# Even mixer's filling weight chunks as split fp32r pieces instead of fp32 tiles

## The reference

```python
def even_mixer(h, w_in, a_qn, a_kn, w_out, top_k):
    aq, ak, av, iq, ik, iw, bq, bk, bv, bg = split_cols(h @ w_in, EVEN_SIZES)
    ...
    ya = dsa_attention(aq, ak, hd(av, A_HEADS), hd(iq, IDX_HEADS), ik, iw, top_k)
    yb = retention(pad_left(hd(bq, B_HEADS)), pad_left(hd(bk, B_HEADS)),
                   pad_left(hd(bv, B_HEADS)))[:, META_PAD:]
    yb = rms_norm_2(yb).astype(h.dtype).reshape(B, L, -1) * jax.nn.silu(bg)
    return jnp.concatenate([ya, yb], axis=-1) @ w_out
```

## Time and profile before

| | us |
|---|---|
| median of 3 runs | 1893.85 (1892.3 to 1895.7) |
| the profiled execution | 1892.15 |
| its span in the trace | 1890.4 |
| TensorE busy | 1860.4 (98%) |
| VectorE busy | 1102.2 (58%) |
| ScalarE busy | 725.6 (38%) |
| TensorE's share of the chain that ended last | 88% |

### The profile page before, as it was taken

One profiled execution on the slowest core, in us unless ns is written; L12 is line 12 of the kernel. 1 busy time (PEld: TensorE's weight loads), 2 busy tenths in 40 slices (PEclk: granted clock), 3 DMA queues, 4 the chain that ended last, 5 costly groups with the idle time before them and its releaser, 6 DMA issues.

```text
span 1890.4 us, 31079 instructions
## 1 busy us (share of the span) xinstructions
PE 1860.4 (98%) x12732; PEld 1686.2 (89%) x12732; DVE 1102.2 (58%) x1752; ACT 725.6 (38%) x928; POOL 0.2 (0%) x4
## 2 busy tenths in 40 slices
PE   9999999999999999999999999999999999999999
PEld 6788999968899999999858558999999999789999
DVE  4556887544588856675344322567556764546763
ACT  3345554224465544333113222433343332334442
POOL 0000000000000000000000000000000000000000
PEclk9999999999999999999999999999999999999999
DMA  5322545424145544554322322345445453144553
GB/s 224 111 112 90 178 178 206 161 98 155 49 140 183 204 176 170 173 179 182 136 99 90 122 112 78 134 170 183 180 166 175 171 194 139 58 162 166 180 211 120
DMA packets 35859, 284.23 MB, mean 150 GB/s; under 512 B 4800, under 2 KB 6976, under 8 KB 8256
## 3 DMA queue, kind: packets, MB, share of 16 engines
q1 hardware_dynamic: 35776, 283.05, 41.8%
HBM read 281.98 MB, written 1.05 MB: 150 GB/s over the span
## 4 chain that ended last, share of the span: by engine, by line
PE 88%; DVE 7%; ACT 4%; issue 1%; DMA 0%; ACTq 0%; DVEq 0%; SPq 0%
PE PS L1192 18%; PE PS L1193 18%; PE PS L1194 18%; PE PS L639 10%; PE PS L648 3%; PE PS L747 3%; DVE split L1757 3%; PE PS L1095 2%; PE PS L616 2%; ACT split L1303 2%; PE PS L719 1%; PE PS L1136 1%; PE PS L662 1%; PE PS L682 1%; PE PS L923 1%
## 5 line engine op out<-in xcount | busy, mean ns | idle before, releaser
L1192 PE MATMUL PS<-Hhi,split 128*128 128x256 f32 (+1 forms) x2080 | 591.7, 284 | 8.6 <-DVE split L1757 7.9
L1757 DVE TENSOR_TENSOR split<-wa,split 128x2048 fp32r<-128x2048 f32 (+1 forms) x174 | 436.9, 2511 | 272.4 <-ACT split L1303 272.4
L1193 PE MATMUL PS<-Hlo,split 128*128 128x256 f32 (+1 forms) x2080 | 591.2, 284 | 0.0
L1194 PE MATMUL PS<-Hhi,split 128*128 128x256 f32 (+1 forms) x2080 | 589.3, 283 | 0.0
L1303 ACT CAST split<-wa 128x2048 fp32r<-128x2048 f32 (+1 forms) x174 | 361.9, 2080 | 145.8 <-PE PS L1194 145.1
L1192 PEld LDWEIGHTS PS<-Hhi,split 128*128 128x128 f32 x2080 | 391.7, 188 | 13.4 <-DVE split L1757 10.7
L1194 PEld LDWEIGHTS PS<-Hhi,split 128*128 128x128 f32 x2080 | 390.9, 188 | 0.0
L1193 PEld LDWEIGHTS PS<-Hlo,split 128*128 128x128 f32 x2080 | 390.6, 188 | 0.2
L1192 PE MATMUL PS<-hidhi,split 128*128 128x256 f32 (+1 forms) x1088 | 310.3, 285 | 6.4 <-DVE hidlo L2333 3.5
L1194 PE MATMUL PS<-hidhi,split 128*128 128x256 f32 (+1 forms) x1088 | 308.9, 284 | 0.0
L1193 PE MATMUL PS<-hidlo,split 128*128 128x256 f32 (+1 forms) x1088 | 308.1, 283 | 0.0
(11 more groups left out here) (283 smaller groups left out, 1696.1 us busy)
## 6 DMA issues: line engine op xcount, KB each, us to landing
wa<-in_wfi SPq DMA_DIRECT2D x126, 1024.0 KB, 4.8
wa<-in_wfo SPq DMA_DIRECT2D x48, 1408.0 KB, 5.8
wa<-in_wmix SPq DMA_DIRECT2D x26, 2048.0 KB, 7.9
wa<-in_wmix SPq DMA_DIRECT2D x4, 1536.0 KB, 6.3
H<-in_wfi SPq DMA_DIRECT2D x3, 1024.0 KB, 10.0
G<-in_wfi SPq DMA_DIRECT2D x3, 1024.0 KB, 4.9
wa<-in_wmix SPq DMA_DIRECT2D x2, 1024.0 KB, 5.9
wa<-in_wmix SPq DMA_DIRECT2D x2, 768.0 KB, 7.5
```

The lines of the kernel that those rows point to most:

```text
L1192: pe.matmul(o, hi, xhi, start=first, stop=False)
L1193: pe.matmul(o, hi, xlo, start=False, stop=False)
L1194: return pe.matmul(o, lo, xhi, start=False, stop=last)
L1757: dve.tensor_tensor(out=wlo[n % 2][:, 0:width], in0=wa[:, c % 2, 0:width], in1=whi[n % 2][:, 0:width].bitcast(F32), op=ALU.subtract).then_ ...
```

## The change

The six filling chunks are computed as split products. The host lays each of them out as four pieces of 8 x 128 columns, so that a piece is contiguous. ScalarE rounds H once into Ehi and VectorE subtracts into Elo, and for each of the 24 pieces ScalarE writes a high half (`round_piece`) into one of three places and VectorE writes the remainder over the weights themselves in wa (`rest_piece`, wa_lo is the same place as wa). TensorE waits for the remainder of the piece and runs `product3` over its 8 tiles: 24 fp32r matmuls. A high half's place is free again when the piece three before has been multiplied. The values are made like the others, channels on partitions, in four tiles of 272 tokens, copied over H by ScalarE and then turned by 12 transposes per group (jobs v0t and v1t). The chunks' order becomes rq, rk, v0, v1, gate0, gate1. The gates and the retention's result lie in RET, the place of QK, since Ehi and Elo take G's and MIX's. The orders of all three engines are rewritten around this. Cut to its core, with part of the indentation taken off deeply nested code:

```diff
-FILL = [(name, i) for name, n in (("rq", 4), ("rk", 4), ("v0", 3), ("turn_q", 4), ("turn_k", 4), ("gate0", 4), ("v1", 3),
-                                  ("gate1", 4)) for i in range(n)]
+FILL = [(name, i) for name, cols in (("rq", range(4)), ("rk", range(4)), ("v0", range(4)), ("turn_q", range(4)),
+                                     ("turn_k", range(4)), ("v1", range(4)), ("v0t", range(3)), ("gate0", range(4)),
+                                     ("gate1", range(2)), ("v1t", range(3)), ("gate1", range(2, 4))) for i in cols]
+SPLIT_EVEN = ("rq", "rk", "v0", "v1", "gate0", "gate1")
-EVEN_FREE = [None, None, None, ("dv_in", 3), None] + [filled(n) for n in ("rq", "rk", "v0", "gate0", "v1", "gate1")] + [None] * 2
+EVEN_FREE = [None, None, None, ("dv_in", 3), None] + [filled(n) for n in SPLIT_EVEN] + [None] * 2
...
+        def over(name, shape):
+            with ExitStack() as shared_place:
+                return shared_place.enter_context(nc.sbuf_tensor(name, shape, F32R))
+        wa_lo = over("wa_lo", [P, 2, KD * 512])
         wa = sb("wa", [P, 2, KD * 512])
...
+        rope_hi = over("rope_hi", [P, KD * P])
         rope = sb("rope", [P, 4, SEQ])
+        own_hi = sb("own_hi", [P, KD * P], F32R)
...
+        with ExitStack() as mix_ctx:
+            mix_ctx.enter_context(nc.sbuf_tensor("mix_head", [P, 4, TT], F32))
+            Elo = mix_ctx.enter_context(nc.sbuf_tensor("Elo", [P, KD, TT], F32R))
         MIX = sb("MIX", [P, 12, TT])
...
+        Ehi, RET = Hhi, QK
+        piece_hi = (split[:].rearrange("p a b -> p (a b)")[:, 10 * P * KD:11 * P * KD], own_hi[:], rope_hi[:])
...
         def ret_out(g):
-            return norm_plan(lane_b2, TT, 4, 0, MIX[:, 4 + 4 * g:8 + 4 * g, :], width=P, post=G[:, 4 * g:4 * g + 4, :])
+            return norm_plan(lane_b2, TT, 4, 0, RET[:, 4 * g:4 * g + 4, :], width=P, post=RET[:, 4 * g:4 * g + 4, :])
...
                     i, bank = FILL[f][1], f % 2
                         pe.wait_ge((S.ring0, S.ring1)[bank], f // 2)
-                    if name in ("v0", "v1"):
-                        mm = tokens(w, 0, 512, RETAINED[i:i + 1], [(bank, 0)])
+                    if name in ("v0t", "v1t"):
+                        last = FILL.index((name[:2], 3))
+                        pe.wait_ge((S.ring0, S.ring1)[last % 2], last // 2 + 1)
+                        pe.wait_ge((S.ring0, S.ring1)[1 - last % 2], (last - 1) // 2 + 1)
+                        t0, tl = RETAINED[i]
+                        for h in range(4):
+                            mm = pe.transpose(PS[0:tl, bank, P * h:P * h + P], H[:, 4 * (name == "v1t") + h, t0:t0 + tl], ident)
                     elif name in ("turn_q", "turn_k"):
                         mm = pe.matmul(PS[:, bank, 0:TT], C("rot", P), lane.QK[:, 4 * (name == "turn_k") + i, :], start=True,
                                        stop=True)
                     else:
-                        mm = tiles(w, [(P * i, P, bank)], TT)
+                        n = 4 * SPLIT_EVEN.index(name) + i
+                        pe.wait_ge(S.ev_lo, n + 1)
+                        hi = piece_hi[n % 3].rearrange("p (k c) -> p k c", k=KD)
+                        lo = wa_lo[:, w, KD * P * i:KD * P * (i + 1)].rearrange("p (k c) -> p k c", k=KD)
+                        for k in range(KD):
+                            mm = product3(PS[:, bank, 0:TT], hi[:, k, :], lo[:, k, :], Ehi[:, k, :], Elo[:, k, :], k == 0,
+                                          k == KD - 1)
                     mm.then_inc(S.fill_in, 1)
                     jobs[0] += 1
+                def slot(c):
+
+                    assert take() == base + c
+                    return (base + c) % 2
...
     def retained(g):
         pe.wait_ge(S.rt_m, upto(S.rt_m))
+        f = FILL.index((f"v{g}t", 2))
+        pe.wait_ge((S.ring0, S.ring1)[f % 2], f // 2 + 1)
+        pe.wait_ge((S.ring0, S.ring1)[1 - f % 2], (f - 1) // 2 + 1)
...
     tiles(use(4, base, KD, 512), [(P * i, P, at + i) for i in range(4)], TT).then_inc(S.prod_done, 1)
-    w = use(5, base, KD, 512)
+    w = slot(5)
+    pe.wait_ge(S.ev_xlo, 1)
     fill("rq", w)
     mean_square(k)
+    fill("rq", w)
     fill("rq", w)
...
     fill("rq", w)
     for a in dsa:
         attend_transposes(a, 0)
-    fill("rq", w)
+    w = slot(6)
+    fill("rk", w)
     for a in dsa:
         attend_scores(a, 1)
-    w = use(6, base, KD, 512)
     fill("rk", w)
     fill("rk", w)
...
-    fill("rk", w)
-    w = use(7, base, KD, 512)
-    fill("v0", w)
+    w = slot(7)
+    for _ in range(3):
+        fill("v0", w)
     for a in dsa:
         attend_transposes(a, 2)
     fill("v0", w)
     for a in dsa:
         pe.wait_ge(S.sm_ptc, upto(S.sm_ptc))
         attend_values(a)
-    fill("v0", w)
     for name in ("turn_q", "turn_k"):
         for _ in range(4):
             fill(name)
-    w = use(8, base, KD, 512)
-    fill("gate0", w)
-    fill("gate0", w)
+    w = slot(8)
+    for _ in range(3):
+        fill("v1", w)
     pe.wait_ge(S.pv_copied, upto(S.pv_copied, 2))
     pe.wait_ge(S.ret_ready, 1)
     decay_scores(0, 0)
-    fill("gate0", w)
+    fill("v1", w)
     decay_scores(0, 1)
+    for _ in range(3):
+        fill("v0t")
+    w = slot(9)
     fill("gate0", w)
     decay_scores(0, 2)
-    w = use(9, base, KD, 512)
-    fill("v1", w)
+    fill("gate0", w)
     retained(0)
-    fill("v1", w)
+    fill("gate0", w)
+    fill("gate0", w)
     mean_square(ret_out(0))
-    fill("v1", w)
-    w = use(10, base, KD, 512)
+    w = slot(10)
+    fill("gate1", w)
     pe.wait_ge(S.nr_rs, upto(S.nr_rs, 0))
-    for kt in range(3):
-        fill("gate1", w)
-        decay_scores(1, kt)
+    decay_scores(1, 0)
+    fill("gate1", w)
+    decay_scores(1, 1)
+    for _ in range(3):
+        fill("v1t")
+    fill("gate1", w)
+    decay_scores(1, 2)
     fill("gate1", w)
     retained(1)
     wo = [use(11, base, 12, 256)]
-    pe.wait_ge(S.ring0, 15)
-    pe.wait_ge(S.ring1, 15)
+    pe.wait_ge(S.ring0, 19)
+    pe.wait_ge(S.ring1, 19)
...
         for j in ks:
-            mm = pe.matmul(PS[:, m, 0:TT], wo[m // 2][:, j, P * (m % 2):P * (m % 2) + P], MIX[:, j, :],
+            mm = pe.matmul(PS[:, m, 0:TT], wo[m // 2][:, j, P * (m % 2):P * (m % 2) + P],
+                           MIX[:, j, :] if j < 4 else RET[:, j - 4, :],
                            start=j == 0, stop=j == 11)
...
         i, bank = FILL[f][1], f % 2
         act.wait_ge(S.fill_in, f + 1)
-        if name in ("v0", "v1"):
-            tl, g = RETAINED[i][1], name == "v1"
+        if name in ("v0t", "v1t"):
+            tl, g = RETAINED[i][1], name == "v1t"
             ins = act.copy(lane.VP[0:tl, i, 4 * g:4 * g + 4, :],
                            PS[0:tl, bank, :].rearrange("p (h d) -> p h d", h=4))
+        elif name in ("v0", "v1"):
+            ins = act.copy(H[:, 4 * (name == "v1") + i, :], PS[:, bank, 0:TT])
         elif name in ("gate0", "gate1"):
-            ins = act.activation(G[:, 4 * (name == "gate1") + i, :], PS[:, bank, 0:TT], ACT.Silu)
+            ins = act.activation(RET[:, 4 * (name == "gate1") + i, :], PS[:, bank, 0:TT], ACT.Silu)
         else:
             ins = act.copy(lane.QK[:, 4 * (name == "rk") + i, :], PS[:, bank, 0:TT])
         ins.then_inc((S.ring0, S.ring1)[bank], 1)
...
+                def round_piece(n):
+
+                    c = base + 5 + n // 4
+                    act.wait_ge(WA[c % 2], 16 * (c // 2 + 1))
+                    if n >= 3:
+                        act.wait_ge(S.fill_in, FILL.index((SPLIT_EVEN[(n - 3) // 4], (n - 3) % 4)) + 1)
+                    at = KD * P * (n % 4)
+                    act.copy(piece_hi[n % 3], wa[:, c % 2, at:at + KD * P]).then_inc(S.ev_hi, 1)
...
         relu()
+    act.copy(Ehi[:], H[:]).then_inc(S.ev_xhi, 1)
+    for n in range(3):
+        round_piece(n)
     product(base + 4)
     squares_of(k)
     filled_tile("rq")
+    round_piece(3)
     roots_of(k)
     filled_tile("rq")
+    round_piece(4)
+    filled_tile("rq")
+    round_piece(5)
     for a in dsa:
         attend_exp(a, 0)
...
         attend_copies(a, 0)
-    filled_tile("rq")
+    round_piece(6)
+    filled_tile("rk")
+    round_piece(7)
...
         attend_exp(a, 1)
     filled_tile("rk")
+    round_piece(8)
     filled_tile("rk")
+    round_piece(9)
     filled_tile("rk")
+    round_piece(10)
...
         attend_exp(a, 2)
-    filled_tile("rk")
-    filled_tile("v0")
+    for n in range(11, 14):
+        filled_tile("v0")
+        round_piece(n)
...
     filled_tile("v0")
-    filled_tile("v0")
+    round_piece(14)
     upto(S.pv_done, 2)
     jobs[0] += 8
-    for _ in range(4):
+    for n in range(15, 19):
+        filled_tile("v1")
+        round_piece(n)
+    for _ in range(3):
+        filled_tile("v0t")
+    for n in range(19, 21):
         filled_tile("gate0")
-    use_exp_and_ln()
-    filled_tile("v1")
+        round_piece(n)
     act.wait_ge(S.rt_pv, 1)
     squares_of(ret_out(0))
-    filled_tile("v1")
+    for n in range(21, 23):
```

(71 more changed lines are left out.)

14 lines of the change are left out of this document (12 added, 2 removed).

## The result

The changed kernel takes 1874.11 us (median of four runs, 1873.53 to 1875.25) against 1894.55 for the kernel before (four runs, 1892.3 to 1895.7): a ratio of 0.9894, 95% interval 0.9881 to 0.9906, so about 20 us less. The forecast was 1876.0, with a range of 1869 to 1885. The profiled execution has a span of 1872.4 us against 1890.4, at a mean granted clock of 0.997.

The account below looks back on a forecast made before the run. TensorE's own stream was taken to bound the even mixer's filled part: 21.9 us shorter, less 4.0 of net waits, gives 17.9 off 1892.15, so 1874.2; with the median 1.7 above the profiled execution, forecast 1876, range 1869 to 1885.

Parts of the forecast that it names:

- The stream: TensorE's work in the even mixer's filled part: fills and value fills of 102.5 us become pieces and transposes of 80.6.
- rival (d): Each fp32r pass on TensorE waits for its own weight load: 108 us more, about 1984 us; chance 0.01.
- the transposes: Added TensorE work turning the values, 12 per group, two groups, at 0.22 us each: 5.2 us.
- The end wait: TensorE stands 2.55 us before the output projection while ScalarE squares the second retention group, then evacuates the last gate tile.
- v0's bank: Third attention block: v0's first tile is evacuated behind long exponentials, so v0's third fill waits about 0.4 us.
- the old 0.6: TensorE's one wait in the mixer before the change, 0.6 us for the normalised keys, forecast to go.
- the surcharge: First fp32r pass after full-precision work takes 0.2 us more; 17 pieces or runs of pieces: 3.4 us.
- From there on 45.7 us follow as before: After the wait before the output projection, the following 45.7 us were to keep their length.
- (a): Less gain: ScalarE's strict order holds pieces up; eleven attention and retention steps losing another 1 us each give 1887; chance 0.09.
- (b): More gain: no surcharge or waits overlap, short last wait; 23.4 us of stream, 2 of waits, below 1871; chance 0.10.
- (c): Slower: the rounding, remainder, fill chain paces TensorE, 2.2 us per exposed piece; 12 exposed give 1902 us; chance 0.05.
- (e): Nothing moves: gain and waits cancel over the run, 1894 us; chance 0.02.

Follow-up runs that it names:

- e2: Changed kernel with each piece as 8 full-precision matmuls again, no roundings, remainders or input split, new value layout and transposes kept: 1889.45 us.
- e1: Changed kernel with ScalarE evacuating the last gate tile before the squares of the second retention group: 1869.47 us.
- e10: Same kernel as e1 (last gate tile evacuated before the squares), measured once more: 1869.62 us.
- e4: Changed kernel with each piece's rounding done twice on ScalarE: 1878.08 us.
- e3: Changed kernel with a second VectorE pass over each remainder before TensorE is told: 1881.19 us.

## Why the prediction was right

**The stream.** Forecast 102.5 to 80.6 us, 21.9 less. The 24 pieces stand in the trace as 17 runs, as forecast, and take 75.8 us in all from the first start of each run to the start of what follows it (less two waits of 0.2), against 72.0 + 3.4 = 75.4. Full loads with every pass cost nothing: passes start 0.125 us apart, so rival (d) is out. The rule of the Trainium skill that stood beside it (page TensorE: Matmul & The Clock Gate, Part 3, The mechanism) doesn't hold here as the prediction read it; the same section also lets a load for the background weight buffer go ahead of matmuls in flight, which the prediction left out. Passes 0.125 us apart with a load record of 0.188 each agree with that reading; no run here shows which buffer a load goes to.

**The mis-sized term: the transposes.** "24 records, two per transpose, took 2.62 us, 0.22 each; 12 per group and two groups are 5.2 us." The row of before was read wrongly: an fp32 transpose is one record, not two. The changed kernel has 24 such records for 24 transposes, and a group of 12 took 1.58 us (1083.49 to 1085.31 less the wait of 0.24), 3.2 in all instead of 5.2. The count of records was in hand and could have been checked against the shape. The 275 ns that the Trainium skill gives for a bf16 transpose inside a kernel (page TensorE: Matmul & The Clock Gate, Part 4) agree with the duration of one fp32 record here, 273 ns. In a run the records overlap: eight took 1.09 us, 0.137 each, and that is the price that a stream pays.
With 75.8 + 3.2 = 79.0 the stream is 23.5 us shorter.

**The waits.** Forecast 4.55 us, measured 3.7. The end wait was forecast at 2.55 and is 2.6, with its place and cause. The 0.4 for v0's bank and the 0.6 for the first rotated tile hardly appear (0.2 at L966). The decays, forecast at 0.7, cost 0.4. The small ones at the value transposes (0.5) were not forecast singly. Less the old 0.6, the waits add 3.1. 23.5 - 3.1 = 20.4 of the 21.4 us measured for the stage. The rest is at unchanged products, counted from their start to the next one's: the two mean squares take 1.63 us each instead of 1.83 and 1.93, the rotations 4.86 instead of 5.13, chunk 4's tiles 14.47 instead of 14.67, and some attention steps 0.1 less each. Mean squares and tiles stand right ahead of a piece, and in e2, where the piece is fp32 again, they take 1.83 twice and 14.67; so more than half of the rest belongs to the hand-over to fp32r, and makes up for a part of the surcharge.

**What the sum left out: the clock.** "From there on 45.7 us follow as before" failed: 47.4 us followed, since TensorE's clock fell behind its own wait. This stall of 2.6 us costs 4.3, shown by taking it away (e1, e10). It is the step that I would now do otherwise: a wait that TensorE gets was priced at its length.

So the stage was 3.5 us shorter than its forecast (141.9, from chunk 4's first product at 987.1 to 1129.0; forecast 163.3 - 17.9 = 145.4, given as "about 145"), and 3.3 us were given back by the clock, half behind the end wait, half ahead of the changed part. The profiled execution was forecast at 1874.2 us and took 1874.18. That agreement is luck in part: two errors of about 3 us with opposite signs. The median was forecast 1.8 higher, at 1876, because the three executions before had a median 1.7 above the profiled one; here the median, 1874.11, lies at the profiled execution.

**The prices on the other engines** held: roundings 1.05 us (forecast 1.0), remainders 1.22 (1.2), the input's remainder 2.42 (2.45). No table load was added: squares and copies between two Silus brought none; there are four loads in the stage, as before. **The rivals:** (a) fell, as no wait but the last is longer than 0.2 us in the table; the order takes 25 us more of ScalarE work at a price of 4 (e4). (b) has it right that the stream saves 23, but not the short last wait, and the surcharge does appear (75.8 - 72.0 = 3.8 us). (c) fell with e3 and e4. (e) fell with the result.

## What to carry to other kernels

Splitting full-precision matmuls into three fp32r passes pays where TensorE bounds the stage and its neighbours have room: here 0.67 us for each piece that takes 3.67, for 2.3 us of ScalarE and VectorE work beside it. Look separately at what a layout wastes: tiles of 16 tokens cost as much as tiles of 128, and turning them took 9.3 us off TensorE's stream. When a change makes TensorE wait, allow for a fall of the clock behind the wait (here 1.6 to 2.9 us more, in some places not in every execution), and look first whether the evacuation that it waits for can be moved ahead of work that nobody waits for.
